# Moving the Newton steps of a head norm to GpSimd and its scaling to ScalarE, in a two-layer decoder trunk

## What is computed

```python
def _rms_norm(x, g):
    xf = xf * lax.rsqrt(jnp.mean(xf * xf, axis=-1, keepdims=True) + RMS_EPS)
    return (xf * g).astype(x.dtype)

def _diff_attention_mixer(...):
    ...
    o = _diff_attention(q, k, v, lam)              # (1, 256, 12 heads, 128)
    o = _rms_norm(o, subln_g) * (1.0 - lambda_init)
```

## Time and profile before

| | us |
|---|---|
| median of 3 runs | 978.69 |
| lowest, highest | 978.06, 979.05 |
| span of the profiled execution, first to last instruction | 976.1 |
| TensorE busy | 951.2 (97%) |
| VectorE busy | 636.7 (65%) |
| ScalarE busy | 469.7 (48%) |
| GpSimd busy | 1.2 (0%) |

### The profile page before, as it was taken

One profiled execution on the slowest core, in us unless ns is written; L12 is line 12 of the kernel. 1 busy time (PEld: TensorE's weight loads), 2 busy tenths in 40 slices (PEclk: granted clock), 3 DMA queues, 4 the chain that ended last, 5 costly groups with the idle time before them and its releaser, 6 DMA issues.

```text
span 976.1 us, 14093 instructions
## 1 busy us (share of the span) xinstructions
PE 951.2 (97%) x5161; PEld 819.9 (84%) x5161; DVE 636.7 (65%) x894; ACT 469.7 (48%) x708; POOL 1.2 (0%) x9
## 2 busy tenths in 40 slices
PE   6999999999999999999999999999999999999995
PEld 5788888888888888888888888888888888888884
DVE  5776656666666666655685465467877878777555
ACT  5756544444444443444464455446445364454441
POOL 0000000000000000000000000000000000000000
PEclk9999999999999999999999999999999999999998
DMA  9665465566666555656567645565565555746552
GB/s 317 222 230 182 136 210 173 184 203 193 194 191 191 186 186 192 210 186 202 166 230 202 189 141 195 169 204 158 176 190 152 177 167 155 198 151 203 198 177 86
DMA packets 149689, 182.30 MB, mean 187 GB/s; under 512 B 8016, under 2 KB 118928, under 8 KB 148880
## 3 DMA queue, kind: packets, MB, share of 16 engines
q1 hardware_dynamic: 148704, 177.25, 57.7%
q10 hardware_dynamic: 944, 4.49, 1.3%
HBM read 176.48 MB, written 2.10 MB: 183 GB/s over the span
## 4 chain that ended last, share of the span: by engine, by line
PE 71%; DVE 14%; DMA 5%; issue 4%; ACT 3%; SPq 2%; DVEq 0%; ACTq 0%
PE psum L340 27%; PE psum L341 13%; PE psum L369 9%; PE psum L368 9%; PE psum L367 9%; DVE lo_ring L794 5%; DMA layer_area<-layer_area 5%; SPq L277 2%; ACT layer_area L758 2%; PE psum L384 1%; DVE layer_area L801 1%; ACT hi_ring L588 1%; DVE psum L1088 1%; DVE layer_area L1065 1%; DVE columns L1092 1%
## 5 line engine op out<-in xcount | busy, mean ns | idle before, releaser
L340 PE MATMUL psum<-hT_split,hi_ring 128*128 128x512 f32 x1600 | 560.1, 396 | 0.0
L794 DVE TENSOR_TENSOR lo_ring<-raw_ring,hi_ring 128x1024 fp32r<-128x1024 f32 x320 | 386.3, 1223 | 240.5 <-ACT hi_ring L588 237.6
L588 ACT ACTIVATE hi_ring<-raw_ring 128x1024 fp32r<-128x1024 f32 x320 | 337.5, 1062 | 403.4 <-PE psum L341 262.1
L341 PE MATMUL psum<-hT_split,lo_ring 128*128 128x256 f32 x1600 | 445.3, 278 | 0.0
L340 PEld LDWEIGHTS psum<-hT_split,hi_ring 128*128 128x128 f32 x1600 | 300.6, 188 | 68.3
L341 PEld LDWEIGHTS psum<-hT_split,lo_ring 128*128 128x128 f32 x1600 | 301.3, 188 | 0.3
L367 PE MATMUL psum<-hi_ring,branchT_split 128*128 128x512 f32 x256 | 100.0, 391 | 0.0
L369 PE MATMUL psum<-hi_ring,branchT_split 128*128 128x512 f32 x256 | 99.7, 390 | 0.0
L368 PE MATMUL psum<-lo_ring,branchT_split 128*128 128x512 f32 x256 | 99.7, 390 | 0.0
L368 PEld LDWEIGHTS psum<-lo_ring,branchT_split 128*128 128x128 f32 x256 | 48.1, 188 | 10.0
L367 PEld LDWEIGHTS psum<-hi_ring,branchT_split 128*128 128x128 f32 x256 | 48.1, 188 | 9.9
(11 more groups left out here) (159 smaller groups left out, 650.7 us busy)
## 6 DMA issues: line engine op xcount, KB each, us to landing
raw_ring<-in_w_in_dram SPq DMA_DIRECT2D x224, 512.0 KB, 4.4
raw_ring<-in_w_out_dram SPq DMA_DIRECT2D x64, 512.0 KB, 4.8
raw_ring<-in_w_kv_mem_dram SPq DMA_DIRECT2D x32, 512.0 KB, 5.3
layer_area<-layer_area SPq DMA_DIRECT2D x48, 64.0 KB, 4.0
stage_area<-in_mem_dram SPq DMA_DIRECT2D x4, 512.0 KB, 7.5
x_residual<-in_x_dram SPq DMA_DIRECT2D x1, 2048.0 KB, 10.9
x_residual<-in_x_dram ACTq DMA_DIRECT2D x1, 2048.0 KB, 8.6
layer_area<-in_post_norm_dram ACTq DMA_DIRECT2D x2, 1024.0 KB, 6.2
```

Of the source, the lines that this page charges most:

```text
L340: mm(o, hi[:, k, P * c:P * (c + 1)], X[:, kt, :], start=kt == 0, stop=False)
L341: last = mm(o[:, SEQ:], lo[:, k, P * c:P * (c + 1)], X[:, kt, 0:SEQ], start=False, stop=kt == KT - 1)
L588: run(whi[:, slot, :], raw[:, slot, :], ACT.Copy).then_inc(hi_ready, 1)
L794: V_.tensor_tensor(wlo[:, slot, :], raw[:, slot, :], whi[:, slot, :].bitcast(f32), SUB)\
```

## The change

The copy of the attention's output to `o_sb` (line 748) goes away; ACT only squares it out of PSUM. DVE does the first three of the 12 small operations (`out_seed`). GpSimd does the three Newton steps, four operations each, every one of which waits for the one before it (`newton`). ACT then scales the four tiles out of PSUM into `o_sb` with the root as a per-row factor (`normalise`). It stands before ACT's unit 1 of the gate group, and for the last pair before unit 1 of the first row group. PE waits for all four. The line numbers of `rsqrt` and below shift by 24 to 27.

```diff
+        def newton(st, p):
+            pool.wait_ge(o_seeded, p + 1)
+            for n in range(3):
+                st.need()
+                st.did(nc.gpsimd.tensor_tensor(o_tmp, o_rstd, o_rstd, ALU.mult))
+                st.need()
+                st.did(nc.gpsimd.tensor_tensor(o_tmp, o_tmp, o_var, ALU.mult))
+                st.need()
+                st.did(nc.gpsimd.tensor_scalar(o_tmp, o_tmp, -0.5, 1.5, ALU.mult, ALU.add))
+                st.need()
+                last = nc.gpsimd.tensor_tensor(o_rstd, o_tmp, o_rstd, ALU.mult)
+                if n < 2:
+                    st.did(last)
+            last.then_inc(o_rstd_ready, 1)
...
         def diff_out_turn(p):
-            pe.wait_ge(on_ready, p + 1)
+            pe.wait_ge(on_ready, p * 4 + 4)
...
         def take_values(p):
             act.wait_ge(pv_done, p + 1)
-            run(o_sb, o, ACT.Copy).then_inc(o_copied, 1)
             for g in range(4):
-                run(o_sq[:, g, :], o[:, g, :], ACT.Square, accum_out=ss[:, 4 + g:5 + g]).then_inc(o_copied, 1)
+                run(o_sq[:, g, :], o[:, g, :], ACT.Square, accum_out=ss[:, 4 + g:5 + g]).then_inc(o_squared, 1)
+
+        def normalise(p):
+            act.wait_ge(o_rstd_ready, p + 1)
+            o = ps[:, 6, :].rearrange("p (g e) -> p g e", g=4)
+            for g in range(4):
+                run(o_sb[:, g, :], o[:, g, :], ACT.Copy, scale=o_rstd[:, g:g + 1]).then_inc(on_ready, 1)
...
-            column_group(G + 2, u + 2 * B_UNITS, s)
+            column_group(G + 2, u + 2 * B_UNITS, s, at={} if first else {1: lambda: normalise(p - 1)})
...
-            out_group(4 + g, U_OUT1 + A_UNITS * g, (G_OUT1 + g) % 2)
+            out_group(4 + g, U_OUT1 + A_UNITS * g, (G_OUT1 + g) % 2, at={1: lambda: normalise(PAIRS - 1)} if g == 0 else {})
...
-        def out_norm(st, p):
-            dve.wait_ge(o_copied, p * 5 + 5)
-            rsqrt(st, o_rstd, ss[:, 4:8], HEAD_DIM, o_eps)
-            st.need()
-            V_.tensor_tensor(o_sb, o_sb, o_rstd.unsqueeze(2).broadcast_to([P, 4, P]), MULT)\
-              .then_inc(on_ready, 1)
+        def out_seed(st, p):
+            dve.wait_ge(o_squared, p * 4 + 4)
+            st.need()
+            st.did(V_.scalar_tensor_tensor(o_var, ss[:, 4:8], 1.0 / HEAD_DIM, o_eps, MULT, ADD))
+            st.need()
+            st.did(V_.tensor_scalar(rs_i, o_var.bitcast(i32), 1, None, ALU.logical_shift_right))
+            st.need()
+            V_.tensor_scalar(o_rstd.bitcast(i32), rs_i, -1.0, float(0x5f3759df), MULT, ADD).then_inc(o_seeded, 1)
```

More of the change, by code:

```diff
@@ L155, in build @@
     y_ss = cols[:, 24:32]
-    rs_v, rs_t, rs_i = cols[:, 32:36], cols[:, 36:40], cols[:, 40:44]
+    rs_v, rs_t, rs_i = cols[:, 32:36], cols[:, 36:40], cols[:, 40:44].bitcast(i32)
+    o_var, o_tmp = cols[:, 86:90], cols[:, 90:94]
     xmax, xnegmax, xsum, xrcp = (cols[:, 44 + 8 * i:52 + 8 * i] for i in range(4))
@@ L199, in build @@
     w_ready, wt_done, wt_ready = sem("weights_ready"), sem("weights_turned"), sem("weightsT_ready")
-    pv_done, o_copied, on_ready, n_done, o_taken = sem("pv_done"), sem("o_copied"), sem("o_normed"), sem("o_turned"), sem("o_taken")
+    pv_done, o_squared, o_rstd_ready = sem("pv_done"), sem("o_squared"), sem("o_rstd_ready")
+    on_ready, n_done, o_taken = sem("o_normed"), sem("o_turned"), sem("o_taken")
     out_ready = sem("out_ready")
-    dve_step = sem("dve_step")
+    dve_step, pool_step, o_seeded = sem("dve_step"), sem("pool_step"), sem("o_seeded")
     X_SCALE, D_SCALE = HEAD_DIM ** -0.5, DIFF_DIM ** -0.5
@@ L312, in _ @@
                                 pattern=[[-1, P]], channel_multiplier=1).then_inc(const_ready, 1)
+        def newton(st, p):
[12 more added lines that the diff above has]
+            last.then_inc(o_rstd_ready, 1)
+        st = Steps(pool, pool_step)
+        for p in range(PAIRS):
+            newton(st, p)
     @block.tensor
@@ L825, in turned, with rsqrt @@
             last.then_inc(tr_lo, 1)
-        def rsqrt(st, dst, total, count, eps=None):
+        def rsqrt(st, dst, total, count):
             w = dst.shape[1]
-            v, t, i = rs_v[:, 0:w], rs_t[:, 0:w], rs_i[:, 0:w].bitcast(i32)
+            v, t, i = rs_v[:, 0:w], rs_t[:, 0:w], rs_i[:, 0:w]
             st.need()
[L832 to L835, removed]
+            st.did(V_.tensor_scalar(v, total, 1.0 / count, RMS_EPS, MULT, ADD))
             st.need()
@@ L1121, in pair @@
                 in_query = {1: lambda: softmax_max(st, p - 1), 2: lambda: softmax_weights(st, p - 1)}
-                in_gate = {0: lambda: out_norm(st, p - 1), 2: rope_keys, 3: lambda: out_take(st, p - 1, 1 - parity)}
+                in_gate = {0: lambda: out_seed(st, p - 1), 2: rope_keys, 3: lambda: out_take(st, p - 1, 1 - parity)}
             in_keys[2] = lambda: rope(st, p * 128 + 64, qT, qrot,
@@ L1131, in _ @@
         pair(st, 0, G_PAIR % 2, 0, first=True)
-        before_pairs, TWO_PAIR_STEPS = st.base + st.n, 2 * (4 + 12 + 1 + 8)
+        before_pairs, TWO_PAIR_STEPS = st.base + st.n, 2 * (4 + 2 + 1 + 8)
         with dve.Fori(1, PAIRS - 1, 2) as p:
@@ L1155, in _ @@
             out_group(4 + g, U_OUT1 + A_UNITS * g, (G_OUT1 + g) % 2,
-                      at={0: lambda: out_norm(st, PAIRS - 1), 4: lambda: out_take(st, PAIRS - 1, 1)}
+                      at={0: lambda: out_seed(st, PAIRS - 1), 4: lambda: out_take(st, PAIRS - 1, 1)}
                       if g == 0 else {})
```

## The result

| | before | after |
|---|---|---|
| median of 6 runs, taken side by side | 978.97 | 994.42 |
| lowest, highest | 978.06, 984.93 | 989.17, 996.5 |
| span of the profiled execution | 976.1 | 987.3 |
| TensorE / VectorE busy | 951.2 / 636.7 | 954.2 / 624.0 |
| ScalarE / GpSimd busy | 469.7 / 1.2 | 472.5 / 21.0 |

The ratio is 1.013 (interval 1.010 to 1.016): the changed kernel is about 13.0 us slower, 10.2 to 15.8. The two medians by themselves lie 15.45 us apart; with the scatter described next, the interval is the safer statement. Forecast was 13.4 slower, 992.1.

A forecast was written before the change was run, and what follows sets the result against it. TensorE, busy 951 of 976 us, and an equally long chain beside it were taken to bound the kernel. Removals gain 0; 11.5 in five pairs plus 1.9 in the last norm on 978.7 gives 992.1, range 983.5 to 1004.5.

The forecast's parts named there:

- A: Start of the seed on VectorE, from which the prediction counts the times of a gate group.
- T: GpSimd's chain of 12 dependent operations after the seed: 0.355 us a step, 4.3 us, entering the total six times.
- loss in five pairs: Keys' rope later by 2.3, 1.6, 2.5, 2.7 and 2.4 us in the five pairs: 11.5 us.
- last norm: Last pair's norm: TensorE transposes at 890.8 in place of 888.93, 1.9 us later.
- What bounds, and the worth of what is removed: TensorE and an equally long chain beside it bound the pairs; removing VectorE's 2.4 us a pair and ScalarE's copy gains 0.
- The wait in ScalarE's queue: Before ScalarE's unit 1 of the gate group: holds VectorE's unit 1 and the rope behind it, to A + 8.3.
- The case on which 992.1 was built: T from 3.4 to 5, GpSimd not held up, TensorE's clock stays: 992.1 us, chance 0.48.
- rival 1: GpSimd's first Newton operation waits for VectorE's unit 0: 1.1 us more a pair, 998.7 us in all; chance 0.30.
- Each delay is passed on whole: Chain from the rope to the next combine unchanged, so every delay of the rope counts in full: 11.5 us.
- Pauses of 3.4 us: TensorE waits before the transposes for ScalarE's scaling, about 3.4 us each time.
- rival 3: TensorE's clock falls in the new pauses, 2.8 us a pair: 992 to 1006; chance 0.10, shared with steps over 0.45 us.
- Rival 2: The transfer before the keys' rope hides the new path, T up to about 1.8: 978.7 us; holds or nearly: chance 0.12.

The follow-up runs named there:

- Experiment 4: Changed kernel with the Newton steps back on VectorE, only the scaling left on ScalarE: 982.08 us, ratio 1.001 to the kernel before.
- Experiments 9 to 11: Kernel before with VectorE reordered: `out_take` ahead of the keys' rope, softmax maximum ahead of unit 0, or both: 975.3, 974.0 and 975.0 us.
- experiment 6: Changed kernel with two Newton steps in place of three: 990.32 us in a single execution.
- experiment 3: Changed kernel with ScalarE's four scalings moved behind its unit 1, before unit 2: 992.33 us, ratio 1.013 to the kernel before.
- experiment 2: Changed kernel with 28 more transposes of a constant ahead of TensorE's wait for the normed output: 994.98 us, ratio 1.015 to the kernel before.
- experiment 8: Changed kernel with only the Newton steps on GpSimd; the `o_sb` copy and VectorE's product stay, ScalarE scales nothing: 994.51 us in one run.
- experiment 7: Changed kernel with four Newton steps in place of three: 1001.47 us in a single execution.

## Why the prediction was right, step by step

| step | predicted | measured |
|---|---|---|
| GpSimd starts | A + 0.60 | A + 0.64 |
| T, its 12 operations | 4.3 | 4.21 |
| step of the chain | 0.355 | 0.28 |
| four scalings | 1.15 | 1.14 |
| transposes | A + 6.1 | A + 6.08 |
| rope | A + 8.3 | A + 8.13 to 8.15 |
| loss in five pairs | 11.5 | 9.35 |
| last norm | 1.9 | 1.83 |
| sum | 13.4 | 11.2 (span), 13.0 (runs) |

- **What bounds, and the worth of what is removed: right.** Experiment 4 took the product off VectorE and gave nothing. Experiments 9 to 11 show that the same wait goes away when the chain is shortened in the right place.
- **The wait in ScalarE's queue: right.** The rope came 8.13 to 8.15 us after the seed in every pair. In experiment 4 the wait stands in the same place and ends 2.5 us sooner, and the rope went back to the transfer; with T alone changed (experiment 6) the rope came sooner by just what T was shorter. In experiment 3, with the wait moved one unit back, it did so too, and then TensorE's pause took over, which the prediction's own working (both within 0.3 us) gives and its list of rivals doesn't.
- **T: the right size from two wrong terms, which is luck.** The case on which 992.1 was built says that nobody is held up and that the clock stays. Neither came true. In fact a step is 0.28 us, 0.075 shorter than taken (12 times: 0.9 less), and in each pair one operation takes 1.13 us in place of 0.20, because VectorE's unit 0 runs beside it (0.9 more). That is the mechanism of rival 1, priced there at 1.1. Without the cancelling, the forecast T would have been off by a microsecond either way, some 6 us of the total. What the Trainium skill says (SBUF — State Buffer, section SBUF: two separate sides), that the two exclude each other for a whole instruction, agrees with the 1.04 to 1.29 us of every held operation beside a unit and 0.20 without one. The term mis-sized was the gap between dependent operations: it was taken as the middle between two gaps at the start of the kernel, 0.165 us, and measured 0.08.
- **"Each delay is passed on whole": not quite.** From the first scores to the last rope the loss was 9.35 us and not 11.5. Of the missing 2.1, 0.75 is the rope at 8.15 in place of 8.3. The other 1.35 is the rest of the chain, which is not as fixed as the prediction took it: the four ways from a keys' rope to the next seed measured 33.8 to 34.1 us before and 33.6 to 34.1 after, 0.9 less in sum, and the way from the first scores to the first seed 0.45 less. On these ways the queries' rope waits for a transfer too, 3.4 to 4.4 us long. That the total still came near 13.4 is luck in part: the profiled executions differ by 11.2 us, and the rest of the 13.0 lies within the scatter of the runs.
- **Pauses of 3.4 us: right in two of five.** Measured were 0.90, 3.54, 1.77, 3.16 and 1.81, and 1.62 in the last norm. Where the clock had fallen after one pause, TensorE came later to the next.
- **Clock falls (rival 3): happened, in two pauses of six, and were not paid for in the pairs.** The scores start 39.5, 43.5, 40.5, 43.3 and 40.5 us apart, the long ones with a fall, but VectorE's maximum starts 42.05, 42.18, 41.72, 41.86 and 41.63 apart: the chain beside TensorE took it up, and with the falls taken away (experiment 2) the pairs were no shorter. The prediction's price was 2.8 us a fall; TensorE itself lost 1.3 to 1.5 us here (spacing less pause) and 1.6 in experiment 8, where the loss was not taken up, and in experiment 7 it reached the last norm.
- **Rival 2** (the cover holds) is out for the change as it is. Experiment 4, with steps of 0.2 us, is the case that it described, and there the cover held (+0.4).

The halves, by the stretch: scaling on ScalarE alone +0.4; Newton steps on GpSimd alone +10.6, of which some 4.8 to 6.4 goes with three falls of the clock; both +11.2. So the loss belongs to GpSimd's slower chain. Where the scalings wait decides how it is paid: in the changed kernel as a longer chain beside TensorE, in the half change as TensorE's pauses and falls. What the half change would cost without falls is only the estimate of experiment 8.

## What to carry to other kernels

When a step moves to another engine, ask first in whose queue the wait for it will stand, and what stands behind that wait. Here it was one weight unit, and behind it a rope on another engine, and each pair lost 2 us by it. Moving the wait alone is not enough if the engine that needs the result then waits as long (experiment 3). Look for the chain that is as long as the busiest engine and ask what on it can go earlier: two swaps in VectorE's order, which take no work off it, gave 0.4%, while the change took 2.1 us a pair off VectorE in a stretch that a transfer ended, and gained nothing by that.

## What the runs showed of the hardware

- GpSimd does a 128 x 4 float32 operation in 0.20 us, and one that depends on the one before starts 0.28 us after that one's start (VectorE: 0.20). The rows at the start of the kernel had given 0.355.
- A GpSimd operation that is issued while VectorE subtracts two SBUF tiles stays until VectorE has ended: 1.04 to 1.29 us in place of 0.20 beside a unit, 0.51 to 0.65 beside the rope's operations on 128 x 512 (experiment 3). Each VectorE unit that falls into the chain adds one such hold. VectorE's own unit took 1.27 and 1.26 in place of 1.23 in two cases (experiments 3 and 8) and was not longer in the others.
- After pauses that the traces give as 1.9 to 5.1 us the clock fell in some cases and in others not: it held in experiment 3 with pauses up to 3.10, and in experiment 6 with pauses up to 2.69. The fall came at the earliest in the pause itself (changed kernel: 1.2 GHz from 730.3, work from 730.83) and at the latest 1.4 us after the work had begun again (experiment 7: work from 820.87, 1.2 GHz from 822.3). The clock stayed at 1.2 GHz for 3.4 us each time (in experiment 8 from 697.0 to 700.4), and twice, in experiment 7, for 6.8. A fall of the short kind took 1.3 to 1.8 us of TensorE's time; in the changed kernel nothing of that shows in the time of the pairs, since another chain set them.
- TensorE can issue 2% fewer matmuls (285 in place of 291 in 50 us) for hundreds of microseconds at a clock of 1.00 without a gap in its records. I know no cause.
